# The expert stage of a two-layer diffusion step: one loop over chunks of tokens, with tokens stationary and split fp32r weights moving

## The reference, cut to what matters

```python
gate_w = g_p * e_p / jnp.sum(e_p, axis=-1, keepdims=True)
expert_ids = g_idx * MOE_PER_GROUP + e_idx
combine = jnp.sum(jax.nn.one_hot(expert_ids, MOE_EXPERTS) * gate_w[..., None], axis=1)
hidden = jax.nn.silu(jnp.einsum('nd,edf->nef', xt, w1)) * jnp.einsum('nd,edf->nef', xt, w3)
y = jnp.einsum('nef,efd->nd', hidden * combine[:, :, None], w2)
```

## Time and profile before

| | |
|---|---|
| three runs | 1867.15, 1873.47 and 1874.77 us, median 1873.47 |
| profiled execution, first to last instruction (its span) | 1869.1 us |
| TensorE busy | 1512.7 us, 81% |
| VectorE, ScalarE, GpSimd busy | 40%, 23%, 11% |
| expert blocks, layer 0 and layer 1 | 768.35 to 1002.57, 1549.65 to 1813.00 us |
| chunks in them | 16 + 2, 16 + 4 |

### The profile page before, as it was taken

The page is one execution under the profiler, slowest core; times in us unless marked ns, Lnnn a source line. Parts: engine busy times, 40 slices in busy tenths (PEclk is TensorE's granted clock), DMA queues, the critical chain, the costliest instruction groups (busy, mean ns, idle before and its releaser), DMA issues. The chain is left out here.

```text
span 1869.1 us, 25731 instructions
## 1 busy us (share of the span) xinstructions
PE 1512.7 (81%) x9767; PEld 1210.8 (65%) x9768; DVE 744.3 (40%) x1388; ACT 427.0 (23%) x832; POOL 214.5 (11%) x166
## 2 busy tenths in 40 slices
PE   2799999656899998499994199989997867999970
PEld 1688888546577445377883199987884446777760
DVE  0412122176477262311113835428993752111118
ACT  0312122142344111011112312125552111101113
POOL 1000000022000032100003500010000321100016
PEclk9899999878999899599997599999998877999995
DMA  7576754701000810559994032220005225877763
GB/s 253 180 233 219 235 194 159 171 12 31 1 1 1 264 65 23 166 206 320 354 354 184 23 94 69 75 63 2 1 1 182 101 90 192 282 262 252 268 217 145
DMA packets 190509, 277.82 MB, mean 149 GB/s; under 512 B 12888, under 2 KB 130352, under 8 KB 190416
## 3 DMA queue, kind: packets, MB, share of 16 engines
q1 hardware_dynamic: 180032, 239.15, 39.0%
q0 software_dynamic: 9520, 34.24, 5.2%
q10 hardware_dynamic: 864, 3.15, 0.4%
HBM read 246.90 MB, written 34.85 MB: 151 GB/s over the span
## 5 line engine op out<-in xcount | busy, mean ns | idle before, releaser
L479 PEld LDWEIGHTS psum<-in_parts 128*128 128x128 f32 x3360 | 410.2, 190 | 58.7 <-issue 58.7
L479 PE MATMUL psum<-in_parts 128*128 128x258 f32 (+1 forms) x3360 | 420.1, 286 | 24.7 <-PEq L324 24.7
L771 PE MATMUL psum<-layer 128*128 128x512 f32 x400 | 174.2, 595 | 2.7 <-PEq L697 2.7
L1775 PEld LDWEIGHTS psum<-layer 128*128 128x128 f32 x1280 | 145.7, 192 | 15.2 <-issue 7.7
L1775 PE MATMUL psum<-layer 128*128 128x128 f32 x1280 | 146.4, 275 | 6.7 <-DVE layer L1980 6.7
L1775 PEld LDWEIGHTS psum<-layer,arena 128*128 128x128 f32 x1152 | 136.3, 198 | 13.2 <-issue 6.7
L1775 PE MATMUL psum<-layer,arena 128*128 128x128 f32 x1152 | 137.0, 282 | 5.3 <-DVE layer L1980 3.7
L771 PEld LDWEIGHTS psum<-layer 128*128 128x128 f32 x400 | 75.9, 191 | 95.6 <-issue 94.1
L563 DVE COPY arena<-psum 128x258 f32<-128x258 f32 (+1 forms) x70 | 29.7, 425 | 238.5 <-PE psum L479 238.5
L1166 PE MATMUL psum<-layer 128*128 128x320 f32 (+1 forms) x384 | 114.1, 434 | 5.4 <-PEq L1356 2.1
L1263 ACT ACTIVATE layer<-psum,layer 128x640 f32<-128x640 f32 (+1 forms) x120 | 84.4, 707 | 118.7 <-DVE layer L1209 118.7
(11 more groups left out here) (298 smaller groups left out, 1870.5 us busy)
## 6 DMA issues: line engine op xcount, KB each, us to landing
arena<-in_moe_w SPq DMA_DIRECT2D x48, 1024.0 KB
layer<-in_moe_w SPq DMA_DIRECT2D x48, 1024.0 KB, 9.5
in<-in_ada_w SPq DMA_DIRECT2D x40, 1024.0 KB, 5.3
y_rows<-layer SPq DMA_DIRECT2D x64, 256.0 KB, 8.2
in<-in_ev_w_in SPq DMA_DIRECT2D x15, 1032.0 KB, 7.6
in<-in_od_w_in SPq DMA_DIRECT2D x11, 1024.0 KB, 5.2
start<-in_ada_w SPq DMA_DIRECT2D x8, 1024.0 KB, 16.5
arena<-mod_rows SPq DMA_DIRECT2D x16, 512.0 KB, 8.2
```

Source lines behind the costliest of these rows:

```text
L479: last = T.matmul(bank(g % W_BANKS)[:, 0:cw], a, b[:, k], start=(k == 0 and m == 0), stop=(k == KD - 1 and m == 2))
L771: last = T.matmul(bank(g % 4), feats[k][:, t * P:(t + 1) * P], wout[:, k, j * BANK:(j + 1) * BANK], start=(k == 0), stop=(k == kt - 1))
L1775: last = T.matmul(dst[:, (2 * f + m) * P:(2 * f + m + 1) * P], weights[m][:, k, f * P:(f + 1) * P], xT[:, k, :], start=(k == 0), stop=(k = ...
```

## The change

The expert block becomes one loop over all chunks (18 and 20 of them here), whatever their expert. For every chunk its expert's weights are loaded, so the further chunks load theirs again. The tokens are stationary now and the weights move: one PSUM bank takes w1 and w3 side by side (512 columns). All products are sums of three fp32r products, and so weights, tokens and hidden units are each split into a high and a low part. The hidden units come out with tokens on partitions and have to be transposed (2 transposes a chunk).

Weights arrive in raw fp32 buffers, one each: two halves of w1 and w3 (`raw_up(0)`, `raw_up(1)`, 1 MiB each) and w2 (`raw_down`, 1 MiB). They are split piece by piece, four pieces j = 0 to 3 for up and two f = 0, 1 for down, each 128 x 1024: ScalarE casts every piece (`split_high`, `split_high_down`); the subtraction is VectorE's for j = 0, 1, 3 and f = 0 and GpSimd's for j = 2 and f = 1. The split parts have one buffer each, so a piece may be cast when TensorE has used that piece of the chunk before (`up_used`), and a raw half is loaded again when its pieces are split. DRAM rows of the weights are read with 4 KB (w1, w3) and 8 KB (w2) in one run, where before they were 1 KB and 4 KB.

```diff
-    def up(dst, weights, xT):
-        for f in range(2):
-            for m in range(2):
-                for k in range(KD):
-                    last = T.matmul(dst[:, (2 * f + m) * P:(2 * f + m + 1) * P], weights[m][:, k, f * P:(f + 1) * P],
-                                    xT[:, k, :], start=(k == 0), stop=(k == KD - 1))
+    def up(q, h):
+        pe.wait_ge(x_high, 2 * q + 1 + h)
+        for k in range(HK):
+            if k % 2 == 0:
+                j = 2 * h + k // 2
...
+            for n in range(2):
+                T.matmul(UP, x_h[:, h * HK + k, :], part_up(n, j)[:, :, k % 2, :], start=(h == 0 and k == 0 and n == 0), stop=False)
+        pe.wait_ge(x_low, 2 * q + 1 + h)
+        for k in range(HK):
+            j = 2 * h + k // 2
+            last = T.matmul(UP, x_l[:, h * HK + k, :], part_up(0, j)[:, :, k % 2, :], start=False, stop=(h == 1 and k == HK - 1))
+            if k % 2:
+                last.then_inc(up_used, 1)
...
+    with pe.Fori(0, m + 1) as p:
+        pe.wait_ge(hid_s, p + 1)
+        up(p + 1, 0)
+        turn_hid(p)
+        turn_x(p + 2)
+        up(p + 1, 1)
+        down(p)
...
+    with act.Fori(0, m + 1) as p:
+        for j in range(2):
+            high_up(p + 1, j)
+        act.wait_ge(hid_s, p + 1)
+        high_hid(p)
+        high_up(p + 1, 2)
+        silu(p + 1)
+        high_x(p + 2)
+        high_up(p + 1, 3)
+        put(p)
+        high_down(p + 1)
...
+    with dve.Fori(0, m + 1) as p:
+        for j in range(2):
+            low_up(p + 1, j)
+        low_hid(p)
+        mult(p + 1)
+        low_x(p + 2)
+        low_up(p + 1, 3)
+        put(p)
+        low_down(p + 1)
```

Four casts of 1024 elements stand ahead of the two exponentials, two behind. GpSimd, which had nothing in this block, subtracts the same six pieces there:

```diff
+    @block.gpsimd
+    def _(pool):
+        for j in range(4):
+            pool.wait_ge(first_high, j + 1)
+            split_low(nc.gpsimd, j).then_inc(first_low, 1)
+        for f in range(2):
+            pool.wait_ge(first_high, 5 + f)
+            split_low_down(nc.gpsimd, f).then_inc(first_low, 1)
```

More of the change, by code:

```diff
@@ L57 @@
 ARENA = 53208
-R = 27824
+R = 27840
 ADA_CW = 512
@@ L1785, in w13_part @@
[L1785 to L1809, removed]
+            o = R
+            xg, yb = at(o, D), at(o + D, D)
@@ L1875, in _, with low_up @@
-                    gather(0, 0)
-                    loop(pool, expert)
-                    pool.wait_ge(o_out, entry(pool, 2, NE - 1) * 16)
+                        pool.indirect_dma_start(out=xg, out_offset=None, in_=h2_rows, in_offset=bass.IndirectOffsetOnAxis(
+                            ap=rows[:, 0:1], axis=0)).then_inc(xg_in, 16)
+                    def low_up(q):
+                        pool.wait_ge(up_high, 4 * q + 7)
+                        split_low(nc.gpsimd, 2).then_inc(up_low_p, 1)
@@ L1957, in _, with high_up, high_x @@
-                    copy_x(0, 0)
-                    loop(act, expert)
+                    def high_up(q, j):
+                        act.wait_ge(up_in[j // 2], 32 * (q + 2))
+                        act.wait_ge(up_used, 4 * q + j + 1)
+                        split_high(act, j).then_inc(up_high, 1)
+                    def high_x(c):
+                        act.wait_ge(turned, c + 1)
+                        if not (isinstance(c, int) and c == 0):
+                            act.wait_ge(up_used, 4 * c)
+                        for b in range(2):
+                            A.copy(x_h[:, b * HK:(b + 1) * HK], TX[:, b * BANK:(b + 1) * BANK].rearrange("p (k n) -> p k n", k=HK)).then_inc(x_high, 1)
@@ L1988, in _, with low_up, low_x @@
-                    copy_x(0, 0)
-                    loop(dve, expert)
+                    def low_up(q, j):
+                        dve.wait_ge(up_high, 4 * q + 5 + j)
+                        split_low(V, j).then_inc(up_low_e if j == 3 else up_low_d, 1)
+                    def low_x(c):
+                        for b in range(2):
+                            dve.wait_ge(x_high, 2 * c + 1 + b)
+                            V.tensor_tensor(x_l[:, b * HK:(b + 1) * HK], TX[:, b * BANK:(b + 1) * BANK].rearrange("p (k n) -> p k n", k=HK),
+                                            whole(x_h[:, b * HK:(b + 1) * HK]), ALU.subtract).then_inc(x_low, 1)
```

406 lines of the change are left out of this document (241 added, 165 removed).

## The result

The changed kernel takes 1903.19 us in the median of four runs (1898.23 to 1904.85), the kernel before 1871.35 in the same series; the ratio is 1.0168 (95% interval 1.0147 to 1.0190). It is slower by 1.7%. All ratios here are of executions in the faster of the chip's two states; one of ten of `double_both_split`, 2774.04 us at a granted clock of 0.74, was in the slower one. The forecast was 1882, or +8.6 us; the profiled executions have spans of 1901.0 and 1869.1 us, +31.9.

What follows compares the result with a forecast made beforehand. TensorE was taken to set the old loop's pace, DMA through single buffers the new one's at 11.7 us a chunk. Expert blocks -5.3 and -11.1, routers 2 x 12.5 gave +8.6: 1882 us, range 1850 to 1912.

Steps and rivals of the forecast that it cites:

- Slower, in the range: Whole kernel: 1882 us, +8.6; range 1850 to 1912 given 0.8, slower by over 0.5% given 0.45.
- the expert blocks, which were to give back 16.4 us: Expert blocks of both layers: 228.9 and 252.3 us against 234.2 and 263.4, so -5.3 and -11.1.
- I add 0.6 us ... and take 11.7 us a chunk: Expert loop: DMA's 11.1 us plus 0.6 for single buffers makes a chunk 11.7 us, bounds 11.0 and 12.4.
- the loop of one raw buffer: Expert loop: landing, casts, subtractions and a 5.2 us reload take 8.5 to 10.9 us, more with a queue in front.
- DMA's 11.1 us: Expert loop: moving 4.19 MB a chunk takes 11.1 us, between 11.8 at 355 GB/s and 10.3 at 408.
- DMA stays at 355 GB/s: Rival for the expert loop: 11.8 us and 0.6 idle make 12.4 a chunk, 1907 us in all; chance 0.22.
- TensorE's 0.23 us a product: Expert loop: each 512-column fp32r product takes 0.23 us, so TensorE works 9.6 us a chunk against 12.05.
- The router's +12.5 a layer: Router block: casts cost 3.2 us and VectorE's waits for GpSimd's subtractions 9.3, +12.5 for each layer.
- the casts' 3.2 us: Router block: four casts ahead of the exponentials make these end at 752.9 instead of 749.75, +3.2 us.
- Start and end: Expert blocks: down of chunk 0 ends near 30 us; second chunk +3, last two -5, last copy +1, nothing in sum.
- The clock rival: Rival for the expert loop: TensorE's waits lower the clock to 0.8, chunk about 14 us, 1965 in all; chance 0.03.
- The four resources: Expert loop: TensorE, ScalarE, VectorE with GpSimd, and DMA each have 8.8 to 11.1 us of work a chunk.

Runs made afterwards that it cites:

- double_both_split: Changed kernel with raw weight and token buffers doubled, router exponentials ahead of the casts, chunk 0's subtractions moved into the expert block; 1871.3 us, ratio 0.9989.
- in_time: `double_both_split` with SyncE's list of loads put in the order in which buffers come free; 1827.0 us, ratio 0.9751.
- in_time_small_pool: `in_time` with GpSimd's two subtractions in the loop taking 64 instead of 1024 elements; 1796.1 us, ratio 0.9601.
- exp_first: Changed kernel with the router block's two exponentials ahead of its four casts, subtractions left in that block; 1903.2 us, ratio 1.0148.
- in_time_two: `in_time` without the products of the low parts of tokens and hidden units, 24 instead of 36 a chunk; 1830.8 us, ratio 0.9758.

## Why the prediction was right or wrong

**Slower, in the range:** right (+31.9 us, range 1850 to 1912), but the size was not: +8.6 was forecast. The sign holds for the reason given only in part: the router's loss was forecast, but the expert blocks, which were to give back 16.4 us, cost 7.7.

**The failed step** is the one that turned DMA's work into a turn: "I add 0.6 us ... and take 11.7 us a chunk". Turns took 12.53 and 12.24, over 16 and 18 full turns 13.3 + 9.7 = 23 us, which is the error. Its mechanism was named (the loop of one raw buffer, "and any queue in front adds"), but the landing was taken from a load with nothing else in the queue, 5.2 us; in the loop it was 8.9, past the 8 us that the prediction had named as a sign of being wrong. With 3.5 for casts and subtractions and 0.2 to issue, the ring is 12.5. What I should have asked is what shares the queues with it in its own turn: the second half of w1 and w3, w2, a gather and the store, 3 MB. (That this traffic makes 8.9 out of 5.2 is the likely reason; no run takes it away alone.)

**DMA's 11.1 us** was not what held. The same bytes pass in 10.8 (`in_time`) and in 10.1 (`in_time_small_pool`), 414 GB/s. The rival "DMA stays at 355 GB/s" gave 12.4 and 1907, and both numbers came close to what was measured. That is luck: its cause, a rate that DMA can't exceed, is refuted; the rate was low because loads were asked for late. The Trainium skill, "DMA: Bandwidth & Descriptors", section "Bandwidth", has about 358 GB/s as the bound of a core, and under "Measured" 425 GB/s for 16 MB on one core alone; the 414 GB/s of this trace are over the first and fit the second.

**TensorE's 0.23 us a product** was right. Eight products of one line of `in_time`:

```profile
L1941 PE MATMUL psum<-moe_parts x8: 389/389/389, 878.6 to 880.2; 128*128 128x512 f32 x8
```

They start 1.6 us apart from first to last, 0.23 each; the 0.39 us shown reach into the next one. My expectations of the first series read 0.26 to 0.27 out of such sums and 11.1 us of work; it is 36 x 0.23 and ten transposes of 0.11 to 0.13, 9.4 to 9.6 us, as the prediction had it.

**The router's +12.5 a layer** was right (11.3 and 12.2), and the port took even instructions of 20 elements, as was chosen. Its split was not: `exp_first` shows that the casts' 3.2 us cost nothing by themselves, since GpSimd's 14 us begin with the first cast wherever it stands. The price is the subtractions' alone.

**Start and end** of the expert blocks came to 1.1 us more than forecast over both layers (24.1 less the 23 of the turns); the router blocks were 1.5 under theirs, and 0.7 lie outside. At the end of layer 0 ScalarE waits until 1016.74 for the last w2 load, and the last copy comes at 1024.45. This load is asked for at 1008.47, just after GpSimd's subtraction has freed the one w2 buffer (1008.24), and takes 8.2 us; in layer 1 it takes 5.4. The last of the 2 MB for `combine` stands ahead of it and lands at 1009.5; what makes up the rest isn't shown.

```profile
1010.80 0.59 ACT L2009 COPY moe<-psum 128x512 f32<-128x512 f32 x1 [2.68 <-DMA y_rows<-moe]
1016.74 1.99 ACT L709 CAST moe_parts<-arena 128x1024 fp32r<-128x1024 f32 x2 [5.35 <-DMA arena<-in_moe_w]
...
1024.45 0.69 DVE L2069 COPY moe<-psum 128x512 f32<-128x512 f32 x1 [4.99 <-PE psum L1961]
```

**The clock rival** is out: the granted clock in the loop was 0.98.

**The four resources:** ScalarE's, TensorE's and the subtractions' work was about right, DMA's too high, and the port between VectorE and GpSimd, with its 9.6 us of work, costs 0.7 us a chunk once the loads come in time, as a collision that delays `low_hid`, not as a sum.

What stays open: how far the kernel before would gain from a load of the first tokens ahead of the 2 MB for `combine` wasn't tried, nor was a split of the six subtractions that keeps GpSimd out altogether. In `in_time_small_pool` ScalarE still waits for the store of the last output (11.4 us in seven times, 880 to 960), so the single output buffer may be the next ring; no run tests it.

## What to carry to other kernels

When work moves from one engine to several, write down for each single buffer its ring (asked for, landed with the turn's own traffic in front, used, free) before any sum of work; the longest ring is the turn. A doubled buffer brings nothing until the queue that asks for its loads has them in the order in which buffers come free. A low DMA rate at a share of 0.94 is no proof that DMA is the bound: ask whether someone waits for a load that could have been asked for earlier.

## What the runs showed of the hardware that I had not expected

Less work for TensorE didn't help, and its clock fell. In `in_time_two` (24 products a chunk) the granted clock is 0.79 in 880 to 960, where `in_time` has 1.00:

```profile
880.00:960.00 80.00, 61.13 (x235) 48.22 (x234) 70.41 (x63) 53.51 (x77) 47.98 (x26) 0.79 0.95 355
```

The chunk is 11.24 us against 10.79 with all 36 products. Within a turn the clock changes level. TensorE stands still for 3.26 us ahead of this down, and in 896 to 902 the granted clock is 0.50, the lower level of 1.2 GHz:

```profile
897.07 3.75 PE L1964 MATMUL psum<-moe_parts 128*128 128x512 f32 x8 [3.26 <-issue]
```

Eight products of down take 3.75 us there, where `in_time` needs 3.01 for twelve after a wait of 1.20, at a granted clock of 1.00. ScalarE then waits for down's result, up to 5.8 us. That this wait is what made the chunk longer is likely, not shown alone.

The port's lock falls on narrow instructions too: 20 elements for 2.34 us beside a subtraction of 1024 on GpSimd, thirteen times their 0.18. The Trainium skill says so too, in "SBUF — State Buffer", section "Who interferes with whom": an instruction of VectorE with two SBUF inputs and one of GpSimd that reads SBUF have one pair of ports, and whoever starts first holds it for its whole instruction. The rows of the router block agree.

The share of busy DMA time doesn't tell how much passes: in `in_time` it is 0.99 with 289 GB/s in 884 to 886 and 1.04 with 424 GB/s in 896 to 898.
